# Six and fourteen gate projections of the merge, computed inside the attention

## What is computed

```python
(..., m_a, m_g, m_s) = split(h @ p['w_in'])
m = (sigmoid(m_a) * (y_attn @ p['w_br_attn'])
     + sigmoid(m_g) * (y_gla @ p['w_br_gla'])
     + sigmoid(m_s) * (y_sgu @ p['w_br_sgu']))
out = m @ p['w_out']
x = layer_norm(ALPHA * x + gate * out)
```

## Time and profile before

| what | us |
|---|---|
| median of 3 runs (1404.79 to 1407.25) | 1406.67 |
| span of the profiled execution | 1402.8 |
| PE busy / DVE / ACT / POOL in that span | 1319.1 / 630.3 / 527.6 / 67.2 |
| layer 0: projections and mixing, merge | 33 to 376, 376 to 607 |
| layer 1: projections and mixing, merge | 640 to 855, 855 to 955 |
| mixer and experts | 980 to 1403 |

### The profile page before, as it was taken

How to read it: one execution, slowest core, us unless ns; L and a number is a source line. 1 busy time by engine, 2 the same in 40 slices (tenths; PEclk the granted TensorE clock), 3 DMA queues, 4 the chain that set the end, 5 groups by cost and what they waited for, 6 DMA issues and landing times. The chain is left out here.

```text
span 1402.8 us, 19345 instructions
## 1 busy us (share of the span) xinstructions
PE 1319.1 (94%) x7958; PEld 1001.5 (71%) x7958; DVE 630.3 (45%) x1095; ACT 527.6 (38%) x887; POOL 67.2 (5%) x92
## 2 busy tenths in 40 slices
PE   6999999899999999998989889999999999999996
PEld 2777676666788888878866679998776566666663
DVE  2323555666233344478336875567413152212222
ACT  2346424444722232325563566443235221111112
POOL 0000002231000000011000230000000000000000
PEclk7999999999999999999999999999999999999999
DMA  9512230327122252224331103564231859999990
GB/s 390 216 61 90 78 127 7 151 91 272 59 90 90 100 200 91 90 91 153 129 113 67 61 32 122 183 220 167 109 120 60 359 196 374 405 410 403 422 384 32
DMA packets 34653, 239.03 MB, mean 170 GB/s; under 512 B 4480, under 2 KB 4736, under 8 KB 6656
## 3 DMA queue, kind: packets, MB, share of 16 engines
q1 hardware_dynamic: 34560, 237.73, 43.8%
HBM read 236.66 MB, written 1.05 MB: 169 GB/s over the span
## 5 line engine op out<-in xcount | busy, mean ns | idle before, releaser
L230 DVE TENSOR_TENSOR pieces_lo<-weight_ring,pieces_hi 128x1024 fp32r<-128x1024 f32 x154 | 187.8, 1224 | 281.2 <-ACT pieces_hi L222 280.9
L248 PE MATMUL proj<-h_hi,pieces_hi 128*128 128x512 f32 (+1 forms) x816 | 288.2, 353 | 7.5 <-DVE h_lo L1159 2.9
L249 PE MATMUL proj<-h_lo,pieces_hi 128*128 128x512 f32 (+1 forms) x816 | 282.0, 346 | 0.0
L250 PE MATMUL proj<-h_hi,pieces_lo 128*128 128x512 f32 (+1 forms) x816 | 281.0, 344 | 0.0
L222 ACT ACTIVATE pieces_hi<-weight_ring 128x1024 fp32r<-128x1024 f32 x158 | 165.4, 1053 | 96.1 <-PE score L250 50.8
L248 PEld LDWEIGHTS proj<-h_hi,pieces_hi 128*128 128x128 f32 x816 | 154.1, 189 | 37.8 <-issue 10.4
L249 PEld LDWEIGHTS proj<-h_lo,pieces_hi 128*128 128x128 f32 x816 | 154.4, 189 | 21.1 <-issue 1.7
L250 PEld LDWEIGHTS proj<-h_hi,pieces_lo 128*128 128x128 f32 x816 | 154.5, 189 | 20.5
L1958 PE MATMUL turn<-expert_parts,e_gathered 128*64 128x256 f32 x768 | 85.3, 379 | 0.8 <-DVE e_gathered L2150 0.8
L1958 PEld LDWEIGHTS turn<-expert_parts,e_gathered 128*64 128x64 f32 x768 | 56.0, 137 | 32.4 <-issue 7.3
L1092 ACT ACTIVATE l_merge_gate<-proj 128x512 f32<-128x512 f32 (+1 forms) x48 | 23.5, 490 | 125.3 <-PE proj L250 125.3
(11 more groups left out here) (442 smaller groups left out, 2038.7 us busy)
## 6 DMA issues: line engine op xcount, KB each, us to landing
weight_ring<-in_stream SPq DMA_DIRECT2D x110, 1024.0 KB, 4.8
expert_parts<-in_experts SPq DMA_DIRECT2D x70, 1024.0 KB, 10.6
weight_ring<-in_experts SPq DMA_DIRECT2D x26, 1024.0 KB, 10.6
l_rows<-in_rows SPq DMA_DIRECT2D x2, 768.0 KB, 15.7
l_y_attn<-in_ada_first SPq DMA_DIRECT2D x1, 1024.0 KB, 5.1
l_y_gla<-in_ada_first SPq DMA_DIRECT2D x1, 1024.0 KB, 7.2
l_y_sgu<-in_ada_first SPq DMA_DIRECT2D x1, 1024.0 KB, 8.1
l_q<-in_ada_first SPq DMA_DIRECT2D x1, 1024.0 KB, 10.0
```

The costliest lines, as they stand in the source:

```text
L230: eng.tensor_tensor(self.part(self.lo_ring[:, n % NPIECE, :], kind), self.raw(slot, c, kind), self.part(self.hi_ring[:, n % NPIECE, :], ki ...
L248: pe.matmul(out, sh, mh, start=start, stop=False)
L249: pe.matmul(out, sh, ml, start=False, stop=False)
L250: return pe.matmul(out, sl, mh, start=False, stop=stop)
```

## The change

Six gates of layer 0 and fourteen of layer 1, the first cells of the merge, become steps `early.0` and so on in the tables, between the softmax units and GLA levels. ACT copies their raw values out of PSUM into a buffer `EG` that the trunk keeps (3584 columns of fp32; six blocks of 512 or fourteen of 256 are used). Two steps `sigmoids.0` and `.1` apply Sigmoid to half of them each, near the table's end. The merge loop leaves those gates out. Both tables are new from end to end, not only where the new steps stand: `ada.0.4` of layer 0 stands earlier, one `merge_gate.s.0` at the end is gone, `ostat`, `orstd`, `ysplit` and `gg` stand in another order. Since some steps now come in another order than their number, semaphore counts are taken from `turn_of`. The space for `EG` comes from a smaller DMA scratch.

```diff
+CELLS = [(b, c) for b in "sag" for c in range(8)]
+EARLY = (6, 14)
+EARLY_W = 3584
...
+    if kind == "early":
+        kind, i = "merge_gate", CELLS[i]
...
-ada.0.4 turn.1 adat.0.4 sv.2 keyt.1 kv.0 kv.1 sv.3 svstat.0 kv.2 score.2 svn.0 pv.0 score.3 sg.0 sums.2 pv.1
...
-pv.13 pairs.13 turn.15 pv.14 ada.1.5 pv.15 adat.1.5 gg.0 query.0 ysplit.s.0 gg.1 out.0 silu.0 ysplit.s.2
-ysplit.s.1 ysplit.s.3 silu.1 out.1 ostat.1 ostat.0 gg.2 ostat.2 gg.3 orstd.1 orstd.2 orstd.0 ostat.3 orstd.3
-silu.3 merge_gate.s.0 silu.2
+ag.0 ag.1 ak.0 gq.0 aq.0 gq.1 stat.0 gate.0 aq.1 ag.2 z.0 aq.2 z.1 ada.0.4 stat.1 rstd.1 z.2 ag.3 rstd.0 aq.3
...
+pv.1 diff.1 sg.2 score.3 diag.0 scale.1 sums.3 turn.2 early.0 pv.2 turn.3 early.1 score.4 early.2 score.5 turn.4
+sums.4 sums.5 sg.3 pv.3 pv.4 pairs.0 diag.1 score.6 diff.2 early.3 scale.2 sums.6 turn.5 score.7 pairs.1 sums.7
...
+score.10 scale.6 sums.10 early.4 adat.1.0 scale.7 pairs.6 pairs.7 diff.8 pv.8 score.11 diff.9 scale.8 turn.10
...
+diff.11 adat.1.1 mix.2 scale.10 turn.12 early.5 ada.1.2 pv.11 pairs.10 turn.13 scale.11 diff.12 pv.12 scale.12
...
+turn.14 pairs.13 sums.15 turn.15 pv.14 query.0 ada.1.5 sigmoids.0 pv.15 mix.3 ysplit.s.0 adat.1.5 ysplit.s.2
+gg.0 silu.0 ysplit.s.1 out.0 sigmoids.1 gg.1 ostat.1 out.1 ostat.0 ostat.2 silu.1 ostat.3 gg.2 ysplit.s.3
+orstd.1 orstd.2 orstd.0 orstd.3 silu.3 silu.2 gg.3
...
+turn.1 svn.0 keyt.1 pv.0 kv.0 kv.1 kv.2 sums.2 diff.0 pv.1 diff.1 early.0 mix.0 diag.0 scale.0 early.1 scale.1
+pairs.0 diff.2 scale.2 score.3 turn.2 diag.1 early.2 early.3 pairs.1 score.4 pairs.2 mix.1 diff.3 diff.4 scale.3
+scale.4 early.4 early.5 pairs.3 diff.5 pv.2 early.6 turn.3 sums.3 score.5 scale.5 pairs.4 turn.4 diff.6 sums.4
+scale.6 pv.3 pairs.5 early.7 diff.7 pv.4 sums.5 pairs.6 score.6 scale.7 diff.8 turn.5 mix.2 early.8 pairs.7
+scale.8 diff.9 early.9 pairs.8 early.10 early.11 scale.9 diff.10 mix.3 scale.10 score.7 turn.6 pairs.9 sums.6
+diff.11 scale.11 pairs.10 pv.5 sums.7 diff.12 turn.7 scale.12 pv.6 pairs.11 diff.13 early.12 scale.13 early.13
+query.0 ysplit.s.1 gg.0 pairs.12 silu.0 gg.1 pairs.13 pv.7 ysplit.s.0 sigmoids.0 silu.1 out.0 ostat.0 ysplit.s.3
+ysplit.s.2 ostat.1 out.1 orstd.0 ostat.3 ostat.2 sigmoids.1 orstd.2 gg.2 gg.3 orstd.1 orstd.3 silu.3 silu.2
...
-        steps += [("merge_gate", x) for x in cells[n + 1:n + 3]] + [("merge", x) for x in cells[n:n + 2]]
+        steps += [("merge_gate", x) for x in CELLS[max(n + 1, EARLY[l]):n + 3]] + [("merge", x) for x in CELLS[n:n + 2]]
...
-    first_use = ("z", 0)
+    first_use = next(s for s in steps if s[0] in ("stat", "z"))
...
+        def early_gate(n):
+            return EG[:, n * NT:(n + 1) * NT]
...
+                elif kind == "early":
+                    act.wait_ge(*PJ.ready(J("early", i)))
+                    act.activation(early_gate(i), PJ.tile(J("early", i))[:, 0:NT], ACT.Copy).then_inc(*PJ.evac(J("early", i)))
+                elif kind == "sigmoids":
+                    first, end = (0, EARLY[l] // 2, EARLY[l])[i:i + 2]
+                    for n in range(first, end):
+                        act.wait_ge(*PJ.evacuated(J("early", n)))
+                    gates = EG[:, first * NT:end * NT]
+                    act.activation(gates, gates, ACT.Sigmoid).then_inc(*sig.early_gates.one())
...
+                    if n == 2:
+                        dve.wait_ge(*sig.y_gla.at(4))
+                    if n < EARLY[l]:
+                        g = early_gate(n)
+                        dve.wait_ge(*sig.early_gates.at(1 if n < EARLY[l] // 2 else 2))
+                    else:
+                        g = SGM[:, n % 4, 0:NT]
+                        dve.wait_ge(*PJ.evacuated(J("merge_gate", i)))
...
-    nc = bacc.Bacc("TRN2", target_bir_lowering=False, num_devices=1)
+    nc = bacc.Bacc("TRN2", target_bir_lowering=False, num_devices=1, dynamic_dma_scratch_size=1024)
```

More of the change, by code:

```diff
@@ L422 @@
[L422 to L426, removed]
@@ new lines @@
+stat.3 z.3 gk.0 stat.2 stat.4 soft.0 av.0 rstd.2 rstd.3 gk.1 rot.2 rot.3 vt.0 gv.0 decay.0 rstd.4 rot.1 gv.1
+gv.2 decay.1 rot.4 rot.0 gv.3 score.0 key.0 sg.0 score.1 keymul.0 turn.0 sv.0 keyt.0 key.1 keymul.1 sv.1 keyt.1
+sums.0 sv.2 sums.1 kv.0 sv.3 svstat.0 adat.0.4 turn.1 svn.0 score.2 kv.1 sg.1 pv.0 sums.2 diff.0 kv.2 scale.0
+pv.1 diff.1 sg.2 score.3 diag.0 scale.1 sums.3 turn.2 early.0 pv.2 turn.3 early.1 score.4 early.2 score.5 turn.4
+sums.4 sums.5 sg.3 pv.3 pv.4 pairs.0 diag.1 score.6 diff.2 early.3 scale.2 sums.6 turn.5 score.7 pairs.1 sums.7
@@ new lines @@
+ada.0.5 pv.5 turn.6 diff.3 score.8 pairs.2 sgsilu.0 scale.3 su.0 diff.4 turn.7 su.1 pv.6 scale.4 sums.8 pairs.3
+mix.0 adat.0.5 diff.5 score.9 scale.5 pairs.4 ada.1.0 turn.8 pv.7 sums.9 diff.6 turn.9 pairs.5 diff.7 mix.1
+score.10 scale.6 sums.10 early.4 adat.1.0 scale.7 pairs.6 pairs.7 diff.8 pv.8 score.11 diff.9 scale.8 turn.10
+su.2 scale.9 pairs.8 score.12 sums.11 pairs.9 ada.1.1 pv.9 turn.11 sums.12 score.13 diff.10 pv.10 su.3 sums.13
+diff.11 adat.1.1 mix.2 scale.10 turn.12 early.5 ada.1.2 pv.11 pairs.10 turn.13 scale.11 diff.12 pv.12 scale.12
@@ L432 @@
+adat.1.2 ada.1.3 score.14 pairs.11 adat.1.3 ada.1.4 diff.13 score.15 sums.14 pairs.12 adat.1.4 scale.13 pv.13
+turn.14 pairs.13 sums.15 turn.15 pv.14 query.0 ada.1.5 sigmoids.0 pv.15 mix.3 ysplit.s.0 adat.1.5 ysplit.s.2
+gg.0 silu.0 ysplit.s.1 out.0 sigmoids.1 gg.1 ostat.1 out.1 ostat.0 ostat.2 silu.1 ostat.3 gg.2 ysplit.s.3
+orstd.1 orstd.2 orstd.0 orstd.3 silu.3 silu.2 gg.3
 """
 ORDER_1 = """
-ak.0 gq.0 gq.1 gate.0 aq.0 z.0 aq.1 stat.1 z.1 aq.2 z.2 aq.3 stat.2 gk.0 gk.1 stat.4 z.3 stat.3 stat.0 soft.0
@@ L442 @@
-diff.7 score.6 scale.7 sums.5 pairs.6 diff.8 turn.5 scale.8 pv.4 pairs.7 diff.9 pairs.8 diff.10 scale.9
-score.7 sums.6 scale.10 pairs.9 turn.6 diff.11 pv.5 sums.7 scale.11 pairs.10 diff.12 scale.12 turn.7 pairs.11
-diff.13 scale.13 pv.6 pairs.12 pv.7 ysplit.s.1 ysplit.s.0 pairs.13 query.0 gg.0 gg.1 ysplit.s.3 silu.0 silu.1
-out.0 ysplit.s.2 out.1 ostat.0 ostat.1 gg.2 ostat.3 ostat.2 gg.3 orstd.0 orstd.2 orstd.1 orstd.3
-merge_gate.s.0 silu.3 silu.2
+aq.0 ak.0 gq.0 aq.1 gq.1 gate.0 stat.1 z.0 aq.2 z.1 rstd.1 stat.2 aq.3 z.2 gk.0 rot.1 stat.4 z.3 rstd.2 stat.3
@@ L523, in trunk_layer @@
     J = lambda name, *i: f"{l}.{name}" + "".join(f".{x}" for x in i)
+    turn_of, number = {}, {}
+    for step in steps:
+        number[step[0]] = number.get(step[0], 0) + 1
+        turn_of[step] = number[step[0]]
     with ExitStack() as ctx:
@@ L727, in _ @@
                     last.then_inc(*PT.done())
-                elif kind in ("sg", "su", "ag", "gg", "aq", "gq", "merge_gate"):
+                elif kind in ("sg", "su", "ag", "gg", "aq", "gq", "merge_gate", "early"):
                     feature_major(J(kind, i), (kind, i))
```

34 lines of the change are left out of this document (12 added, 22 removed).

## The result

The changed kernel takes 1372.32 us (median of 4 runs, 1371.17 to 1375.71) where the kernel before takes 1406.24 beside it (1404.79 to 1407.25). The ratio is 0.9761, 95% interval 0.9747 to 0.9775: 33.9 us faster, and the profiled spans differ by 33.4 (1402.8 and 1369.4 us).

What follows compares the result with a forecast made beforehand. PE was taken to bound the kernel, with only its attention waits to gain. Fills of -9.7 and -9.4 us plus merge heads of +4.5 and +1.0 gave -13.6: 1406.7 to 1393 us, range 1377 to 1409.

Steps and rivals of the forecast that it cites:

- What bounds the kernel: Whole kernel: PE, busy 94% of the span, is the limit; only its waits can be gained, and DVE stays below it.
- the attention windows: 220 to 345 us (layer 0) and 780 to 836 (layer 1): PE idle 12.1 and 11.8 us, 23.9 together.
- the rest of the tables: New step orders before the attention windows: no net effect, taken at 0, bounds -6 and +5 us.
- The 1.9 us for ada.0.4: Layer 0, ada.0.4 moved to just before ag.3: PE waits some 1.9 us for its copy and split.
- The fill in layer 0: Layer 0 attention window: early gates fill four fifths of 12.1 us idle PE time, 9.7 us.
- the upper bound by PEld: Both attention windows: raising the weight-load share to the dense merges' gives 46.2 us of room, 25.7 and 20.5.
- The fill in layer 1: Layer 1 attention window: early gates fill four fifths of 11.8 us idle PE time, 9.4 us.
- Rival 1: Attention windows: more is filled than PE's busy time admits, -31.4 us, 1375 us; chance 0.17.
- The head of the merge: Between gg.3 and the first merges: less cover for the norm costs +4.5 us in layer 1, +1 in layer 0.
- Layer 1's merge: 14 merges without gates between: PE and DVE work equal at 2.9 us per pair, so hidden; bounds 0 and +2.
- POOL beside DVE: Layer 1 window: added two-input splits contend with POOL; multiplies 0.10 us longer each, chain gains 2.8 us at most.
- The rigid shift: After the trunk: its gain reaches the end whole; span and median move alike, 3.9 us apart.

Runs made afterwards that it cites:

- tables_only: Both new tables without early gates and sigmoids steps, all gates back in the merge, against the kernel before: 1394.26 us, ratio 0.991.
- gates_only: Old tables with the 6 and 14 early gates put at the same kinds of neighbour, against the kernel before: 1407.6 us, ratio 1.0005.
- gates_bunched: Changed kernel with layer 0's six early gates in one block behind turn.2: 1380.78 us, ratio 0.9808 to the kernel before.
- waits_no_split: Old tables, six layer 0 gates directly ahead of PE's longest waits, fed without weight splits, against the kernel before: 1399.06 us, ratio 0.9954.
- head_mended: Changed kernel with layer 1's second Sigmoid beside the first and orstd.0 behind all squares: 1368.51 us, ratio 0.973 to the kernel before.

## Why the prediction was wrong in size

**What bounds the kernel: right, but read in the wrong stretches.** PE's waits were what there was to gain, the dense merges shrank by what left them (183.6 to 166.8, that is 16.8 for three gates at 5.57), and DVE never became the limit: 62.79 busy in 84 us is a share of 0.75, where I expected near 0.8. But I called 220 to 345 and 780 to 836 "the attention windows" and took 12.1 and 11.8 us of idle time from them. The whole attention stretches hold 21.2 and 22.1 us. In layer 0 the new table reaches all of it: the earlier trace rows showed the 7.8 us of 80 to 220, which I then put under "the rest of the tables" and priced at nothing, and 1.2 are left. In layer 1 the 9 to 10 us ahead of the gates stayed. I also misread the second row: L707 is the ada product itself, waiting for a turn bank that ACT's copy of the turned probabilities frees. The waits of adats and turns for ACT's copy of the ada result (L936) are the next rows of that same view, 2.2 and 1.9 us, and they are the kinds of wait that the distance bears on.

**The rest of the tables: the step that failed.** Taken at 0, bounds -6 and +5; tables_only measured -12.7, outside the bounds. The bounds were drawn from the idle time of the early stretches alone, and nothing in the working asked what the moved adats do; their distance is worth 17 to 19 us in these tables. The 1.9 us for ada.0.4 did not appear: the longest wait for a split in 80 to 220 is 0.9 us.

**The fill in layer 0: right in size by luck.** Predicted 0.8 x 12.1 = 9.7 us. Layer 0's attention came out 28.0 us below its work, of which the tables alone give 17.9 and the gates on top 10.1. That 10.1 stands so near to 9.7 is luck, for a condition was missing: at the same kinds of neighbour in layer 0's old table the gates filled nothing (gates_only), in one block in the new table they filled nothing either (gates_bunched), and directly ahead of the old table's waits they brought a gain only without their splits (waits_no_split). 17.4 of the 28.0 us are idle time; the other 10.6, inside the busy time, I had only as the upper bound by PEld.

**The fill in layer 1.** Predicted 9.4, measured 13.6, and 14.1 against the same table without gates: 12.4 of idle time (0.56 of 22.1) and 1.2 inside busy. The window that I had cut was filled almost wholly; 751 to 835 has 0.3 us idle left. So here the share was too small, by 4 to 5 us.

**Rival 1** was the case that came true in its number (1375 us) and partly in its reason: 11.8 us of the 41.6 filled were inside what I had called busy. The Trainium skill ("Perfetto Trace Analysis", Identifying the Most-Contended Engine) holds the LDWEIGHTS share to be the better measure, and by it I had 46.2 us of room, of which 41.6 were filled. That is nearer than my 23.9, but the gates alone filled 24.2 of the 41.6, and the measure does not carry over to the whole stretches: the PEld rule on the whole stretches gives 319.2 - 220.54 / 0.81 = 46.9 and 203.6 - 147.92 / 0.995 = 54.9 us, 102 in all, more than twice what was filled, while the plain idle time of the whole stretches is 43.3. Here the stretch mattered more than the view, and the order of the steps more than either.

**The head of the merge.** Predicted +4.5 in layer 1, measured +3.9 (+2.5 beside tables_only), by the chain that I gave: fewer matmuls between out.1 and the merge, three more table loads, a Sigmoid of 1.70 us (1.7 predicted) in ACT's queue; head_mended takes it away and gains 3.8. The wait was to be some 6 us; it was 4.0, and it ended otherwise than I had it. I expected it ahead of the second merge, for a score bank that DVE frees; it stood ahead of the first, and what came last was the low part of a weight piece, queued behind that chain. Layer 0 +1, measured +0.2, and -3.3 beside tables_only, whose own order makes a split late there.

**Layer 1's merge.** Predicted 0, bounds 0 to 2; measured +3.6. I had compared PE's and DVE's work, and they do fit. What I left out is the clock, see below: of the 3.6 us 0.8 are idle time, and some 2.5 are an estimate for the 5 us at half clock.

**POOL beside DVE.** The fear cost nothing. POOL's multiply has 764 ns as before, and DVE's became shorter, 445 where it was 517, with 16 two-input splits in the stage instead of 2 (the kernel after, 751 to 835):

```profile
L1303 DVE TENSOR_TENSOR l_decayed<-l_decayed,l_gla_q 128x256 f32<-128x256 f32 x14 | 6.2, 445 | 2.6 <-ACT l_decayed L1089 2.5
```

The means hide something. In the kernel before most of DVE's 14 multiplies take 0.40 to 0.43 us, and three take 0.73 to 0.95. Those three are the ones that overlap a POOL multiply for more than half a microsecond. One such pair, by the timelines of DVE and of POOL:

```profile
819.03 0.94 DVE L1279 TENSOR_TENSOR l_decayed<-l_decayed,l_gla_q 128x256 f32<-128x256 f32 x1
818.87 0.82 POOL L1389 TENSOR_TENSOR l_decayed<-l_decayed,l_gla_k 128x256 f32<-128x256 f32 x1 [0.22 <-ACT l_decayed L1074]
```

In the kernel after one multiply of DVE's overlaps so, and it takes 0.76 us; the others take 0.42 or 0.43. So the contention that the Trainium skill describes ("GPSIMD Engine Reference", Key points) is in both traces. The change made it no worse, because its splits hardly meet POOL: 11 of the 16 do not overlap it at all, the one that does for 1.3 us takes 1.26, and the longest takes 1.35 where 1.22 is usual.

**The rigid shift.** It held: the trunk is 33.7 us shorter (952.8 to 919.1 at the end of layer 1's merge), the span 33.4. The 3.9 us that I put around the span compare two executions; in one and the same it is 1.8 (1371.17 and 1369.4).

**The sum, as measured.** The forecast was -9.7 - 9.4 + 4.5 + 1.0 = -13.6. Beside tables_only the same terms are -10.1 and -14.1 for the fills, +2.5 and -3.3 for the heads, and +3.6 - 0.1 for the merges: -21.5. The tables alone are -12.5, where I had 0, and both are the -34.0 of the stretches. Of the miss of 20 us 12.5 are the tables' and some 8 the gates'.

**What stays open.** The distance of the adats and the places of the gates are shown as causes in the new tables. Why the new table's places fit, when the old table's places beside the same kinds of step do not, was not taken apart further: the spread of sg, su and svn and the spacing of score and turn were not tried by themselves, nor were long distances in the old table. The division into tables and gates holds for the way over tables_only; on the way over gates_only the gates bring nothing first and the tables all of it then. How much of the 10.6 us inside busy time is the clock and how much modelled ends is an estimate, 6 to 7 us, from the granted clock.

## What to carry to other kernels

In this kernel filler in an in-order queue was worth something only where it stood between a producer and the step that waits for it, where its own inputs and bank were ready at that point, and where the other engines' order let them use the time. The first is shown by gates_bunched, the second by waits_no_split; the third is what is left to explain gates_only and is argued. Without them 33 us of dense work left PE's idle time as it was (17.5 and 17.1 us). With them the gates took 10.1 us out of layer 0's attention, beside the 17.9 that the order alone had brought. When an order of work is new as a whole, price its distances between producer and consumer and sum idle time over the whole stage, not over the stretch in which the new blocks stand.

## What the runs showed of the hardware

**A 4 us wait can cost more than itself, because of the clock.** Within the 4.0 us in which PE had nothing to do at the head of layer 1's merge the granted clock fell to half (1.2 GHz), and it stayed there for 6.8 us. Short stretches of the kernel after show it:

```profile
848.00:851.00 3.00, 0.49 (x5) 0.29 (x3) 0.48 (x1) 2.97 (x4) 0.00 (x0) 0.95 0.00 0
851.00:854.00 3.00, 1.51 (x7) 1.54 (x8) 2.84 (x4) 2.97 (x6) 0.00 (x0) 0.50 0.00 0
854.00:857.00 3.00, 3.00 (x16) 3.00 (x16) 1.68 (x3) 1.60 (x3) 0.00 (x0) 0.50 0.72 268
857.00:860.00 3.00, 3.00 (x25) 3.00 (x25) 2.25 (x7) 1.68 (x3) 0.00 (x0) 0.91 0.20 82
```

PE is busy all through 854 to 857 and does 16 matmuls there, against 25 in the next 3 us. In the timeline starts are 0.21 us apart at 853 and 0.12 at 857.8.

In head_mended that wait is gone, both stretches have a clock of 1.00, and the merge is 1.5 us shorter beside the head's 3.1. There is no fixed price: after the 3.9 us wait of the same trace that ends at 699.9 the clock is 0.76 in 699 to 702, 0.67 in the next 3 us and then 1.00, and the 3.0 us wait in layer 0's head of tables_only stands in a stretch with 1.00. A view that counts slow matmuls as busy time hides the loss; PEclk beside the busy share shows it.

**A table switch costs its load and no more.** Each load takes 1.28 us and the next activation starts 0.01 to 0.02 us after its end (841.57 + 1.28 = 842.85, start 842.87), so a switch is worth 1.3 us in a chain.
